# Differential attention: least scores of negated queries, placed between the mixes of a head's two token blocks

## The reference

```python
def diff_attend(qb, keys, vals, lam):
    s = jnp.einsum('bqhmd,bkhmd->bhmqk', qb, keys).astype(F32) * (DIFF_HD ** -0.5)
    p = jax.nn.softmax(s, axis=-1)
    a = p[:, :, 0] - lam * p[:, :, 1]
    return jnp.einsum('bhqk,bkhe->bqhe', a.astype(vals.dtype), vals)
...
    yl = diff_out(ol, subln, lam_init, w_out)     # root-mean-square norm per head, then the output matrix
```

## Time and profile before

| what | value |
|---|---|
| time, median of 3 runs | 2203.34 us (2203.25 to 2204.33) |
| the profiled execution | 2202.43 us, its span 2200.7 us |
| PE busy over the span | 2143.6 us, 97% |
| DVE busy | 1310.2 us, 60% |
| ACT busy | 612.8 us, 28% |
| POOL busy | 186.0 us, 8% |
| heads 0 to 7 of the attention, with the value sums before and the first output tiles behind | about 1884 to 1951 us of the span |

### The profile page before, as it was taken

The page is one execution under the profiler, slowest core; times in us unless marked ns, Lnnn a source line. Parts: engine busy times, 40 slices in busy tenths (PEclk is TensorE's granted clock), DMA queues, the critical chain, the costliest instruction groups (busy, mean ns, idle before and its releaser), DMA issues.

```text
span 2200.7 us, 35715 instructions
## 1 busy us (share of the span) xinstructions
PE 2143.6 (97%) x14043; PEld 1831.0 (83%) x14043; DVE 1310.2 (60%) x2210; ACT 612.8 (28%) x1632; POOL 186.0 (8%) x268
## 2 busy tenths in 40 slices
PE   6999999999999999999999999999999999999998
PEld 4788888888855888888888888888888888579998
DVE  3577756367865784467775536676642444745564
ACT  3111110133445886411111114111111321642211
POOL 2100000000023450000000000000000011000000
PEclk9999999999999999999999999999999999999999
DMA  9555554233320001235554323555523234024463
GB/s 349 190 168 175 169 149 114 53 103 102 90 77 21 3 3 40 77 106 177 167 181 125 110 72 102 166 156 169 154 66 106 77 96 141 31 73 152 158 180 89
DMA packets 244527, 260.58 MB, mean 118 GB/s; under 512 B 6841, under 2 KB 224563, under 8 KB 244275
## 3 DMA queue, kind: packets, MB, share of 16 engines
q1 hardware_dynamic: 222643, 181.23, 26.9%
q0 software_dynamic: 21760, 77.61, 11.2%
HBM read 255.67 MB, written 1.05 MB: 117 GB/s over the span
## 4 chain that ended last, share of the span: by engine, by line
PE 91%; DVE 4%; ACT 2%; DMA 2%; issue 1%; POOL 0%; DVEq 0%; SPq 0%; ACTq 0%; POOLq 0%
PE bank L987 42%; PE bank L1121 21%; PE bank L1223 6%; PE bank L831 4%; PE bank L951 2%; PE bank L1663 2%; PE bank L1344 1%; PE bank L1278 1%; PE bank L1583 1%; DMA big<-in_w_mod 1%; PE bank L1355 1%; PE bank L808 1%; PE bank L796 1%; PE bank L1459 1%; PE bank L1446 1%
## 5 line engine op out<-in xcount | busy, mean ns | idle before, releaser
L987 PE MATMUL bank<-hs,ring 128*128 128x256 f32 (+1 forms) x2112 | 444.0, 354 | 4.0 <-ACT hs L1947 3.0
L987 PEld LDWEIGHTS bank<-hs,ring 128*128 128x128 f32 x2112 | 363.0, 190 | 52.3 <-issue 8.3
L1121 PE MATMUL bank<-big,ring 128*128 128x256 f32 (+1 forms) x1888 | 380.7, 360 | 0.0
L1121 PEld LDWEIGHTS bank<-big,ring 128*128 128x128 f32 x1888 | 331.2, 190 | 39.8 <-issue 0.9
L987 PE MATMUL bank<-room,big 128*128 128x256 f32 (+1 forms) x1408 | 296.0, 353 | 0.0
L987 PEld LDWEIGHTS bank<-room,big 128*128 128x128 f32 x1408 | 242.3, 191 | 26.6
L2565 DVE SCALAR_TENSOR_TENSOR mring<-mring,cond 128x1024 f32<-128x1024 f32 x196 | 240.1, 1279 | 7.8 <-DMA mring<-in_w_mod 7.8
L987 PE MATMUL bank<-room,ring 128*128 128x256 f32 (+1 forms) x704 | 149.3, 355 | 2.5 <-ACT room L1988 1.8
L694 POOL DMA_DIRECT2D mring<-in_w_mod x112 | 59.2, 529 | 994.1 <-DVE mring L2559 468.9
L987 PEld LDWEIGHTS bank<-room,ring 128*128 128x128 f32 x704 | 121.0, 190 | 20.0 <-ACT room L1988 6.8
L1992 ACT ACTIVATE room<-room 128x256 f32<-128x256 f32 (+1 forms) x88 | 34.4, 390 | 293.6 <-DVE room L2771 293.6
(11 more groups left out here) (417 smaller groups left out, 3209.7 us busy)
## 6 DMA issues: line engine op xcount, KB each, us to landing
ring<-in_ffn_w_in SPq DMA_DIRECT2D x88, 1024.0 KB, 5.7
mring<-in_w_mod POOLq DMA_DIRECT2D x124, 512.0 KB, 3.9
ring<-in_ffn_w_out SPq DMA_DIRECT2D x32, 1408.0 KB, 7.1
ring<-in_gdn_w_in SPq DMA_DIRECT2D x16, 1024.0 KB, 5.7
ring<-in_diff_w_in SPq DMA_DIRECT2D x12, 1024.0 KB, 5.3
big<-in_w_mod POOLq DMA_DIRECT2D x19, 512.0 KB, 11.2
ring<-in_gdn_w_out SPq DMA_DIRECT2D x4, 1024.0 KB, 5.2
ring<-in_diff_w_out SPq DMA_DIRECT2D x4, 1024.0 KB, 5.2
```

The costliest lines, as they stand in the source:

```text
L987: last = mm(bank[:, (g0 + b) % 4, 0:width], w[:, k, jj * P:(jj + 1) * P], rhs[:, k, 0:width], start=start and k == 0, stop=(k == KC // 2 - ...
L1121: last = mm(bank[:, (go + b) % 4, 0:width], w[:, k, :], rhs(k), start=start and k == 0, stop=(k == FH - 1), skip_group_check=True)
```

## The change

Four things are edited. (1) ACT's copies of the eight query tiles out of PSUM (L2282) multiply by minus one eighth, so the scores come out negated and scaled. (2) DVE takes the minimum of each score row in place of the maximum, and the instruction that multiplied by minus one eighth (L3339) is gone; the exponential takes the minimum as its bias with scale minus one. (3) The mix loses the small product with lambda (L3348): the first wide instruction now multiplies the second map by two per-partition numbers (its reciprocal and minus lambda), and the second one adds the first map times its reciprocal. (4) The lists of DVE and ACT are re-ordered. On DVE the first two minima of the next head stand between the mixes of a head's two blocks. On ACT the exponentials of the next head are cut in two parts: block 0 between the two copies of `copy_a`, block 1 where all four were, and `root` moves behind the second copy. The lists of PE, POOL and SP are the same as before.

```diff
-                        fn(big[:, q, 0:LAT], bank[:, g % 4, 0:LAT], ACT.Copy).then_inc(S["acc_freed"], 1)
+                        fn(big[:, q, 0:LAT], bank[:, g % 4, 0:LAT], ACT.Copy, scale=-HALF ** -0.5).then_inc(S["acc_freed"], 1)
...
-                            fn(probs[n % 2][:, k, :], bank[:, 4 + k, :], ACT.Exp, bias=st[:, 4 + k:5 + k], scale=HALF ** -0.5,
+                            fn(probs[n % 2][:, k, :], bank[:, 4 + k, :], ACT.Exp, bias=st[:, k:k + 1], scale=-1.0,
...
                         copy_a(h, (0,))
+                        if more:
+                            exps(h + 1, (0, 1))
+                        copy_a(h, (1,))
                         if h:
                             root(h - 1)
-                        copy_a(h, (1,))
                         if more:
-                            exps(h + 1, range(4))
+                            exps(h + 1, (2, 3))
                         leave(h)
...
-                            steps.link(v_.reduce_max(st[:, k:k + 1], bank[:, 4 + k, :], AX_X))
-                            v_.tensor_scalar(st[:, 4 + k:5 + k], st[:, k:k + 1], -HALF ** -0.5, None, ALU.mult
-                                             ).then_inc(S["max_done"], 1)
-
-                    def mix(h):
+                            v_.tensor_reduce(st[:, k:k + 1], bank[:, 4 + k, :], axis=AX_X, op=ALU.min).then_inc(S["max_done"], 1)
+
+                    def mix(h, ts=range(2)):
...
-                            steps.did(v_.tensor_scalar(st[:, 16 + t:17 + t], st[:, 13 + 2 * t:14 + 2 * t], lamv[:, 5:6], None, ALU.mult))
...
-                            steps.link(v_.tensor_scalar(amix[:, t, :], pr[:, 2 * t, :], st[:, 12 + 2 * t:13 + 2 * t], None, ALU.mult))
-                            v_.scalar_tensor_tensor(amix[:, t, :], pr[:, 2 * t + 1, :], st[:, 16 + t:17 + t], amix[:, t, :],
+                            steps.link(v_.tensor_scalar(amix[:, t, :], pr[:, 2 * t + 1, :], st[:, 13 + 2 * t:14 + 2 * t], lamv[:, 5:6],
+                                                        ALU.mult, ALU.mult))
+                            v_.scalar_tensor_tensor(amix[:, t, :], pr[:, 2 * t, :], st[:, 12 + 2 * t:13 + 2 * t], amix[:, t, :],
...
-                    mix(0)
+                    mix(0, (0,))
...
-                        maxima(h)
-                        mix(h)
+                        maxima(h, (0, 1))
+                        mix(h - 1, (1,))
+                        maxima(h, (2, 3))
+                        mix(h, (0,))
+                    mix(HEADS - 1, (1,))
```

More of the change, by code:

```diff
@@ L3337, in maxima @@
                             of("scores_done", n, 4, k + 1)
-                            steps.link(v_.reduce_max(st[:, k:k + 1], bank[:, 4 + k, :], AX_X))
-                            v_.tensor_scalar(st[:, 4 + k:5 + k], st[:, k:k + 1], -HALF ** -0.5, None, ALU.mult
-                                             ).then_inc(S["max_done"], 1)
-                    def mix(h):
+                            v_.tensor_reduce(st[:, k:k + 1], bank[:, 4 + k, :], axis=AX_X, op=ALU.min).then_inc(S["max_done"], 1)
+                    def mix(h, ts=range(2)):
                         st, pr = stat[h % 2], probs[h % 2]
-                        for t in range(2):
+                        for t in ts:
                             of("probs_done", h, 4, 2 * t + 2)
                             steps.link(v_.reciprocal(st[:, 12 + 2 * t:14 + 2 * t], st[:, 8 + 2 * t:10 + 2 * t]))
-                            steps.did(v_.tensor_scalar(st[:, 16 + t:17 + t], st[:, 13 + 2 * t:14 + 2 * t], lamv[:, 5:6], None, ALU.mult))
                             if h:
                                 of("a_turned", h - 1, 2, t + 1)
-                            steps.link(v_.tensor_scalar(amix[:, t, :], pr[:, 2 * t, :], st[:, 12 + 2 * t:13 + 2 * t], None, ALU.mult))
-                            v_.scalar_tensor_tensor(amix[:, t, :], pr[:, 2 * t + 1, :], st[:, 16 + t:17 + t], amix[:, t, :],
+                            steps.link(v_.tensor_scalar(amix[:, t, :], pr[:, 2 * t + 1, :], st[:, 13 + 2 * t:14 + 2 * t], lamv[:, 5:6],
+                                                        ALU.mult, ALU.mult))
+                            v_.scalar_tensor_tensor(amix[:, t, :], pr[:, 2 * t, :], st[:, 12 + 2 * t:13 + 2 * t], amix[:, t, :],
                                                     ALU.mult, ALU.add).then_inc(S["mixed_done"], 1)
```

## The result

The changed kernel takes 2215.64 us (median of 4 runs, 2214.93 to 2217.07) against 2203.3 us (4 runs): 12.3 us slower, a ratio of 1.0056 with a 95% interval of 1.0044 to 1.0068. Slower was forecast, with 8.45 us more; the range held the time, near its upper end. The profiled execution took 2215.82 us, 13.4 more than the one of before, and its span is 2214.1 us.

The account below looks back on a forecast made before the run. A ring of waits between DVE and PE was taken to set the head-loop turn: 2.47 (start) + 6.30 (six turns) - 0.32 (end) = +8.45 us, so 2211.8 against 2203.34; range 2208.8 to 2216.4.

Parts of the forecast that it names:

- The ring: Head loop: waits between DVE and PE from second mix to second mix, 7.53 us a turn against 6.48.
- The start and the end: Head loop's start: head 0's second mix waits for head 1's first minima, +2.47 us; its end, fewer late exponentials, -0.32.
- the squares of head 6: PE at the head loop's end: expected some 8.4 us later than 1932.42, as a sign of being right.
- The wide product with two numbers per partition: DVE's mix: 512 columns priced at 0.545 us, or about 0.68 if a second number halves the pace.
- Two minima: DVE's score rows: a minimum priced as a maximum, 0.61 us from one to the next, 1.22 for two.
- the clock at 1.00 throughout: PE: the granted clock was to stay at 1.00, 2.4 GHz, as a sign of being right.
- Rival C: Head loop: PE's waits of about 1.7 us lower the clock, +4.6 us per turn hit, 2216.4 to about 2244; chance 0.08.
- Rival A: Head loop: DVE's own work decides, turn 5.6 us, seven turns save 6 us, 2197.3; chance 0.07.
- Rival B: Head loop: DVE's own round sets the turn, 7.21 us, 2209.9; floor of the slow case, no separate chance.
- Rival D: Head loop: no change, the new order costs what the dropped instructions save, 2203.3; chance 0.05.

Follow-up runs that it names:

- the first experiment: The changed kernel with DVE's and ACT's lists in the order of before, cheaper instructions kept: 2203.02 us against 2203.89, ratio 0.9998.
- DVE's order alone: The changed kernel with ACT's list in the order of before, DVE keeping its new order: 2215.98 us against 2203.76, ratio 1.0059.
- `attend` out of the ring: The changed kernel with PE's scores of block 0 of head h+2 ahead of attend(h): 2210.08 us against 2203.76, ratio 1.003.
- the order alone: The kernel before with the new DVE and ACT lists and the old instructions: 2221.16 us against 2203.89, ratio 1.0081.
- ACT's order alone: The changed kernel with DVE's list in the order of before, ACT keeping its new order: 2205.23 us against 2203.89, ratio 1.0007.
- filled: The changed kernel with three unread 128x256 products in PE's wait, heads 0 to 6: 2212.22 us against 2203.89, ratio 1.0039.

## Why the prediction was right, and where it was short

*The ring.* Right in each part: mix to turn 0.81, to scores 0.58, to `attend` 1.06, to the scores of block 0 1.92, to the minima 1.16, to the next second mix 1.98 (1.21 + 0.19 + 0.58, 1905.23 to 1907.21). The sum of these is 7.51, against 7.53 forecast. That DVE's list made it and ACT's did not is shown by the two experiments that undo one list each; that PE's list is the other half of it, by the one that takes `attend` out.

*The start and the end.* From head 1's first scores to its second ones it is 4.52 us now and 2.08 before, +2.44 (forecast +2.47). From the last scores to the squares of head 6 it is 4.03 us (forecast 4.01).

*The instructions.* The wide product with two numbers per partition takes 546 ns (forecast 545). Groups of DVE's instructions by line and shape:

```profile
L3340 DVE TENSOR_REDUCE room<-bank 128x1 f32<-128x512 f32 x32 | 20.6, 685 | 23.1 <-PE bank L1656 23.1
L3350 DVE TENSOR_SCALAR room<-room,lamv 128x512 f32<-128x512 f32 x8 | 4.4, 546 | 0.3
```

From 410 ns for 256 columns to 546 for 512 is 0.53 ns a column, as steep as the form with one number (0.52), so the second number did not halve the pace. The Trainium skill gives a float32 tensor_scalar within SBUF twice the plain rate ("VectorE: DVE Perf Modes", the perf-mode tier table). The trace bears that out for the form with two numbers: a float32 operation on two tensors took 1.06 ns a column in the kernel before (416 ns for 256 columns, 687 for 512), twice the 0.53. Two minima take 1.29 us together, 0.61 from one to the next; a minimum is no dearer than a maximum was (685 ns against 684).

*The clock: the step that failed.* Of the signs that were named for being right, "the clock at 1.00 throughout" did not come, and the squares of head 6 came 13.54 us later, not 8.4. Rival C was set aside with "the gaps are as long as the one that did no harm", and given 0.08, as a case instead of the ring. The clock fell besides the ring, in three of six turns. One gap of 1.70 us in another stage was not enough to call gaps of that length harmless: of the six waits of 1.74 and 1.75 us in the changed kernel, two were followed by the lower clock and four were not. The prediction's own walk of the start also holds a longer wait, of some 2.2 us up to the turn at 1891.12, which was not weighed; it measured 2.23, and the clock fell behind it too. The price was wrong the other way: 4.6 us per turn supposed all of PE's part of the ring at the lower level, and it measured 1.65, since the clock came back while `attend` ran.

Ring and clock together make the 13.54 us at the squares of head 6: 0.25 (the stage began that much later) + 2.44 (the start) + 6 x 1.035 (the turn, 7.51 against 6.475) + 3 x 1.65 (the clock) - 0.30 (the end) = 13.55.

*The range held the time partly by luck.* The ring without the clock was forecast up to 2214, and 2215.64 lies above that. The room up to 2216.4 stood for one turn at the lower clock at 4.6 us. There were three in the profiled execution, at 1.65 each, 4.95 in all: too few turns and too high a price nearly cancelled.

*Rival A* (DVE's work decides) fell with the first experiment. DVE was busy for 5.99 of 6.50 us, and relieving it by 0.9 us brought 0.04 us a turn, because the ring through ACT's root and PE was hardly shorter; with the root moved, the turn fell to 5.97. By the Trainium skill's rule for the most-contended engine ("Perfetto Trace Analysis", section Identifying the Most-Contended Engine), the engine with the highest occupancy is the one to optimize first. In this turn that rule alone did not find the gain. *Rival B* was not the bound here; it came out, at 7.17 us, once `attend` was taken from the ring. *Rival D* is refuted by the turn of 7.51.

*What stays open:* why the clock fell in three turns, one behind a wait of 2.23 us and two behind 1.75, and did not in the others, behind the same 1.75. The length of one wait does not decide it. At the start of the stage the clock fell behind 2.23 us in the changed kernel, and stayed at 1.00 behind 2.22 us in two others (DVE's order alone, `attend` out of the ring) and behind 2.67 us in a third (the order alone). The profiled executions show only that where every turn has a wait of 1.7 us or more, two to four of the seven were followed by the lower clock, and that where the turns have waits of at most 1.07 us (ACT's order alone), 0.84 (`attend` out of the ring) or 0.46 (filled), none was.

## What to carry to other kernels

Before moving an instruction between two others, write down for the partner engine what stands in its list between the release and the answer: an instruction moved *into* that round trip is nearly free as long as it fits, and one that waits for a *later* answer pulls all of the partner's list up to that answer into the ring. Where several engines are nearly as busy as the busiest (here 5.99, 5.83 and 5.22 of 6.50 us), shortening the busiest one helps only as far as the next ring, so sum the second-longest ring before pricing the gain. And when a gain per turn does not arrive in the total, look at the hand-over behind the loop: here a root moved for the loop's sake was what the first step after the loop waited for.

## What the runs showed of the hardware

That a turn with a 1.75 us wait on PE can bring the granted clock to 0.50 for some 3 us, in some turns and not in others, was not expected; nor that a wait of 2.67 us left it at 1.00 where one of 2.23 did not; nor that 1.46 us of products that nobody reads, put into that wait, make a program 3.4 us faster (2215.64 to 2212.22).
